# Regrouping the expert row gathers of a hybrid decoder step: U rows of the next slot ahead of the V rows of this one

## The chip, the cores and the metric

The kernel runs on one core of a Trainium2 chip. The metric is the device time in microseconds (us), the median of several runs. Engines are called as the profile calls them: PE (TensorE), DVE (VectorE), ACT (ScalarE), POOL (GpSimd), SP (SyncE).

## The reference

One decoder layer for 512 prompt tokens and 32 sample tokens (8 sequences of 4), model width 1024, everything in f32. Attention and retention are computed in parallel branches, the sample's attention over 4096 cached positions held in pages. What the change touches is the channel mixer behind them, in which each token picks 16 of 16384 experts for each of 8 heads and reads a row of 4 KB from each of two tables for every pick:

```python
def peer_block(h, w_q, sub_keys, u_tab, v_tab):
    ...
    s1, i1 = lax.top_k(s[:, :, 0], PEER_TOPK)
    s2, i2 = lax.top_k(s[:, :, 1], PEER_TOPK)
    ...
    top, flat = lax.top_k(cand, PEER_TOPK)
    e = ...
    g = jax.nn.softmax(top, axis=-1)
    u = u_tab[e]
    act = jax.nn.gelu(jnp.einsum('thkd,td->thk', u, h).astype(F32))
    return jnp.einsum('thk,thkd->td', (g * act).astype(h.dtype), v_tab[e])
```

At the end of the layer each token's x is gated: `x + sigmoid(rms_norm(x) @ w_ple_gate) * (p_emb @ w_ple)`.

## The kernel before

**Slots.** The expert work is cut into 34 slots (`SLOTS`): 8 for each of the four prompt tiles of 128 tokens (`BLOCKS`; one slot holds one head's or an equal share of picks), 2 for the 32 sample tokens. A slot is 16 gathers of U rows and 16 of V rows. Each gather (`gather`, L2127) is one indirect DMA of 128 rows of 4 KB, 512 KB, into one of 16 buffers (`ring`). The row numbers are columns of `IDX`.

**What a slot does.** DVE finds the top 16 (`dve_topk`). ACT makes the softmax's exponentials (`act_softmax`). PE turns the numbers and gates so that picks lie on partitions (`pe_turn_index`) and ACT copies them out of PSUM (`act_keep_index`). When a U row group has landed, DVE multiplies it with the hidden rows and sums (`dve_dots`, L2038, one call for each buffer). `dve_weights` makes gelu and gate into 32-column weight matrices `DG` (L2061), with one exponential from ACT in between (`act_gelu`, L2104; DVE waits for it at L2056). PE multiplies them with the V rows (`pe_weigh`, L2117), 16 matmuls for each of four groups `a` of four buffers, and adds into PSUM banks 6 and 7 over the eight slots of a tile; `dve_add` (L2073, L2075) adds these to x in `XB`.

**The ring.** In each buffer U(i), V(i), U(i+1), V(i+1) follow one another. V row group j of slot i is issued when dot j of slot i is done (`u_used`), the U rows of slot i+1 four at a time when weighing group a of slot i is done (`v_used`). All gathers stand in one queue, POOL's, in program order: 16 of V, then 16 of U. Among them at a block's end are the 16 small loads of h rows (`load_h_rows`, L2125), which wait for the store of h2 (L2173).

**The background.** Everything else, from the projections of later tiles to the sample's attention, is a generator on each engine (`pe_mixer`, `dve_mixer`, `act_mixer`), wrapped in `Background`. Each of its steps has a due position in slots (`STAGE_UNITS`, `PARTS_OF_TIME`, `when`): group 1 lies at -0.3 to 5.95, group 2 with the sample's retention at 6.02 to 14.2, the sample's attention over the cache (stage D, L794, L805, L865) at 14.25 to 26, the rest of the sample at 26.05 to 29.95. `mixer.until(s)` emits on this engine all steps due up to s, and then the slot's own work follows. So the positions set each engine's program order and nothing else: an engine does its instructions in that order and waits on semaphores where it has to.

PE before, for slot i: weighing group a at i + 0.1 + 0.1a, turning the index of slot i+2 at i + 0.5. DVE: weights at i, top-k of slot i+2 at i + 0.05, dot j of slot i+1 at i + 0.2 + 0.04j, the add of a finished tile at dot 10 (i + 0.6). ACT: exponential at i, softmax at i + 0.05, index copy at i + 0.5, store of a finished x at i + 0.65.

**The gating** of tile t (`pe_gating`, L1079 to L1108) has positions too (`GATE_SLOT`), 7 units for each tile: tile 0 at 30.1, tile 1 at 31.0, tile 2 at 32.0, tile 3 at 32.9 to 33.5, the sample (PT) at 33.7 to 33.9. Tile 3 and the sample need the sums of slots 31 and 33.

Of the kernel before, what the change touches and what calls it, by code (L numbers as in the profile page):

```python
# [209 lines left out]
GATE_SLOT = {0: (30.1, 31.0), 1: (31.0, 32.0), 2: (32.0, 32.9), 3: (32.9, 33.5), PT: (33.7, 33.9)}  # L210
# [40 lines left out]
def bass_decoder_step(nc, ins, outs, consts):  # L251
# [5 lines left out]
    with ctx:  # L257
# [48 lines left out]
        IDX = small(2, TOPK).bitcast(I32)  # L306
# [1671 lines left out]

        def first_of(i):
            return i == BLOCKS[BLOCK_OF[i]][1][0]  # L1980
# [50 lines left out]
        def dve_dots(dve, i, between):  # L2031
            p, blk = i % 2, BLOCK_OF[i]
            for j, (g, a) in enumerate(U_ORDER):
# [3 lines left out]
                dve.wait_ge(row_in[j], i * 32 + 16)  # L2037
# [50 lines left out]
        def act_keep_index(act, i):  # L2088
# [3 lines left out]
            act.activation(IDX[:, p, :].rearrange("p (g a) -> p g a", g=4), src[:, :, 0, :], ACT.Copy).then_inc(idx_put, 1)  # L2092
# [13 lines left out]
        def pe_weigh(pe, i, a):  # L2106
# [6 lines left out]
            for g in range(4):  # L2113
                pe.wait_ge(row_in[4 * a + g], i * 32 + 32)
# [12 lines left out]
        def gather(pool, table, i, j, g, a):  # L2127
            pool.indirect_dma_start(ring[j], None, table, bass.IndirectOffsetOnAxis(ap=IDX[:, i % 2, 4 * g + a:4 * g + a + 1], axis=0)  # L2128
                                    ).then_inc(row_in[j], 16)

        SMALL_LOADS = 10
        with nc.Block() as block:
# [207 lines left out]
            def _(pool):  # L2340
# [4 lines left out]
                for j, (g, a) in enumerate(U_ORDER):  # L2345
                    gather(pool, u_rows, 0, j, g, a)
                for i in range(SLOTS):
                    ends = last_of(i) and i + 1 < SLOTS
                    if ends:
                        t = BLOCKS[BLOCK_OF[i] + 1][0]  # L2350
                        pool.wait_ge(h2_stored, 16 * GROUPS[LATE_IN[t]].ln)
                    for j, (g, a) in enumerate(V_ORDER):
                        pool.wait_ge(u_used, i * 16 + j + 1)
# [3 lines left out]
                    if i + 1 < SLOTS:  # L2357
                        pool.wait_ge(idx_put, 2 * (i + 1) + 2)
                        for j, (g, a) in enumerate(U_ORDER):
                            if j % 4 == 0:  # L2360
                                pool.wait_ge(v_used, 4 * i + j // 4 + 1)
                            gather(pool, u_rows, i + 1, j, g, a)

            @block.tensor
            def _(pe):
# [5 lines left out]
                for i in range(SLOTS):  # L2371
                    for a in range(4):
                        mixer.until(i + 0.1 + 0.1 * a)
                        pe_weigh(pe, i, a)
                    if i + 2 < SLOTS:
                        mixer.until(i + 0.5)
                        pe_turn_index(pe, i + 2)
                mixer.until(SLOTS)

            @block.vector  # L2380
            def _(dve):
# [7 lines left out]
                for i in range(SLOTS):  # L2389
                    def between(j):  # L2390
                        mixer.until(i + 0.2 + 0.04 * j)
                        if j == 10 and last_of(i):
                            dve_add(dve, i)
# [7 lines left out]
                    else:  # L2401
                        dve_add(dve, i)
                mixer.until(SLOTS)

            @block.scalar
            def _(act):
# [14 lines left out]
                for i in range(SLOTS):  # L2421
# [3 lines left out]
                    if i + 2 < SLOTS:  # L2425
                        mixer.until(i + 0.05)
                        act_softmax(act, i + 2)
                        mixer.until(i + 0.5)
                        act_keep_index(act, i + 2)
# [42 lines left out]
```

## Time and profile before

| | |
|---|---|
| median of 3 runs | 2755.46 us (2750.58 to 2759.26) |
| profiled execution, own time | 2745.58 us |
| its span | 2743.5 us |
| PE, DVE, POOL busy | 1814.7, 1276.4, 1296.6 us |
| moved by DMA | 913.48 MB, mean 333 GB/s |
| gathers | 544 of U and 544 of V |

"Idle before, releaser" in a row of the trace is the time for which the engine stood still before the instruction and what ended it. Busy time of PE is what the profiler shows of pipelined matmuls. A wait is listed as the waiting engine and line, an arrow, and what released it.

### The profile page before, as it was taken

The numbers are of one execution on the slowest core, as the hardware profiler recorded it, in microseconds if no ns is written. First come the engines' busy times: TensorE is split into PE (matmuls) and PEld (weight loads), VectorE is DVE, ScalarE is ACT, GpSimd is POOL, SyncE is SP. The second block draws the span as 40 slices with busy tenths as digits, with TensorE's granted clock in tenths as the row PEclk, the third lists the DMA queues.
The fourth block names the chain that finished last, engine by engine and source line by source line (L and its number), as shares of the span: only waits on it lengthen the run. The fifth ranks groups of instructions, "written<-read, shape, count | busy, mean of one in ns | idle before, by whom it ended". The sixth has DMA issues, their size and how long they took to land.

```text
span 2743.5 us, 31504 instructions
## 1 busy us (share of the span) xinstructions
PE 1814.7 (66%) x10482; PEld 864.7 (32%) x10482; DVE 1276.4 (47%) x3210; ACT 497.6 (18%) x1061; POOL 1296.6 (47%) x1172
## 2 busy tenths in 40 slices
PE   6987687898965934787556666556665643364747
PEld 3443343343433412222233343333333310011212
DVE  1106664535354664644435354244342554664551
ACT  2112221101121100211122222222221200011121
POOL 0014634425545563645464542345235567876760
PEclk8998899999986965898878777767776766587878
DMA  6888958889968897999899999899899999999992
GB/s 210 279 263 308 388 182 337 312 302 368 396 241 293 314 359 270 367 355 398 340 347 380 383 342 343 322 397 355 316 350 356 361 402 386 384 405 405 346 375 79
DMA packets 338178, 913.48 MB, mean 333 GB/s; under 512 B 36865, under 2 KB 46242, under 8 KB 337378
## 3 DMA queue, kind: packets, MB, share of 16 engines
q0 software_dynamic: 160512, 580.99, 56.0%
q1 hardware_dynamic: 175250, 324.59, 33.2%
q10 hardware_dynamic: 2256, 5.90, 0.6%
q8 instruction: 85, 1.39, 0.2%
q14 instruction: 75, 0.61, 0.1%
HBM read 894.82 MB, written 16.52 MB: 332 GB/s over the span
## 4 chain that ended last, share of the span: by engine, by line
DMA 26%; PE 16%; POOL 8%; SPq 6%; issue 5%; DVE 4%; ACT 1%; DVEq 0%; ACTq 0%; POOLq 0%
DMA arena<-in_cache_v_dram 10%; POOL arena L2128 8%; DMA arena<-in_cache_k_dram 4%; SPq L2178 3%; PE ps L467 3%; SPq L2183 3%; PE ps L2117 3%; DMA arena<-in_peer_w_q_dram 3%; PE ps L794 2%; PE ps L1108 2%; DMA arena<-in_peer_u_dram,arena 2%; DMA arena<-in_peer_v_dram,arena 2%; PE ps L865 2%; DMA out_ret_sample_dram<-arena 2%; DMA arena<-in_w_in_dram 1%
## 5 line engine op out<-in xcount | busy, mean ns | idle before, releaser
L2128 POOL DMA_INDIRECT arena<-in_peer_u_dram,arena x544 | 615.3, 1131 | 994.2 <-PE ps L2117 804.8
L2038 DVE CUSTOM_DVE_ANT_0 arena<-arena 128x1024 f32<-128x1024 f32 x544 | 656.0, 1223 | 544.3 <-DMA arena<-in_peer_u_dram,arena 536.3
L467 PE MATMUL ps<-arena 128*128 128x512 f32 (+1 forms) x1472 | 686.9, 620 | 85.5 <-DMA arena<-in_peer_w_q_dram 30.9
L2128 POOL DMA_INDIRECT arena<-in_peer_v_dram,arena x544 | 640.6, 1178 | 202.9 <-issue 163.4
L467 PEld LDWEIGHTS ps<-arena 128*128 128x128 f32 (+1 forms) x1472 | 275.5, 193 | 471.0 <-issue 343.2
L2117 PE MATMUL ps<-arena 128*32 128x512 f32 x2176 | 322.3, 715 | 146.5 <-DMA arena<-in_peer_v_dram,arena 124.2
L794 PE MATMUL ps<-arena 128*128 128x128 f32 x1024 | 195.8, 353 | 209.5 <-DMA arena<-in_cache_k_dram 155.2
L794 PEld LDWEIGHTS ps<-arena 128*128 128x128 f32 x1024 | 154.8, 182 | 298.9 <-DMA arena<-in_cache_k_dram 158.5
L865 PE MATMUL ps<-arena 128*32 128x512 f32 x512 | 101.5, 876 | 152.6 <-DMA arena<-in_cache_v_dram 152.6
L1258 ACT ACTIVATE arena<-ps 128x512 f32<-128x512 f32 x256 | 143.4, 593 | 282.8 <-PE ps L794 282.5
L2117 PEld LDWEIGHTS ps<-arena 128*32 128x32 f32 x2176 | 71.5, 124 | 327.3 <-issue 300.9
L2125 POOL DMA_DIRECT2D arena<-h_for_experts x80 | 40.6, 523 | 188.4 <-DMA h_for_experts<-arena 188.4
L686 PE MATMUL ps<-arena 128*128 128x128 f32 (+1 forms) x360 | 57.6, 301 | 99.3 <-DVE arena L1920 34.5
L2056 DVE TENSOR_SCALAR arena<-arena 128x16 f32<-128x16 f32 x34 | 5.9, 175 | 219.1 <-ACT arena L2104 219.1
L805 PE MATMUL ps<-arena 128*32 128x128 f32 x2048 | 100.6, 360 | 1.3 <-ACT arena L1258 0.7
L686 PEld LDWEIGHTS ps<-arena 128*128 128x128 f32 (+1 forms) x360 | 46.1, 163 | 140.3 <-issue 66.9
L805 PEld LDWEIGHTS ps<-arena 128*32 128x32 f32 x2048 | 74.2, 145 | 20.8 <-issue 9.4
L1108 PE MATMUL ps<-arena 128*128 128x512 f32 (+1 forms) x160 | 72.1, 604 | 0.0
L865 PEld LDWEIGHTS ps<-arena 128*32 128x32 f32 x512 | 13.0, 129 | 173.8 <-DMA arena<-in_cache_v_dram 152.1
L2092 ACT ACTIVATE arena<-ps 128x16 int32<-128x16 f32 x34 | 6.3, 184 | 295.5 <-PE ps L2084 295.5
L477 PE MATMUL ps<-arena 128*32 128x512 f32 x288 | 50.6, 640 | 13.0 <-DMA arena<-in_w_a_up_dram 13.0
L1904 DVE TENSOR_TENSOR arena<-ps,arena 128x512 f32<-128x512 f32 (+1 forms) x20 | 13.7, 687 | 88.2 <-PE ps L467 88.2
(214 smaller groups left out, 1636.8 us busy)
## 6 DMA issues: line engine op xcount, KB each, us to landing
arena<-in_w_in_dram SPq DMA_DIRECT2D x156, 512.0 KB, 7.5
arena<-in_cache_k_dram SPq DMA_DIRECT2D x256, 256.0 KB
arena<-in_cache_v_dram SPq DMA_DIRECT2D x256, 256.0 KB
arena<-in_peer_w_q_dram SPq DMA_DIRECT2D x64, 512.0 KB, 12.6
arena<-in_w_out_dram SPq DMA_DIRECT2D x32, 512.0 KB, 10.1
arena<-in_w_b_up_dram SPq DMA_DIRECT2D x24, 512.0 KB, 6.6
arena<-h_for_experts POOLq DMA_DIRECT2D x80, 128.0 KB, 13.4
arena<-in_peer_u_dram,arena POOLq DMA_INDIRECT x544, 9.4
```

Source lines behind the costliest of these rows:

```text
L467: last = pe.matmul(bank[0:rows(t), :], x[:, c, cs], weight(pe, g.no, name, c), start=(c == 0), stop=(c == nd - 1))
L686: last = pe.transpose(bank[:, k * P:k * P + n], src[0:n, k * P:(k + 1) * P], ident[0:n, 0:n])
L794: last = pe.transpose(ps[:, hp % 2, k * P:(k + 1) * P], KP[i % 2][:, k, hp * P:(hp + 1) * P], ident)
L805: last = pe.matmul(ps[32 * k:32 * k + 32, 2, r * P:(r + 1) * P], Qb[:, p // 2 % 2, hp, :], KPT[:, r % 2, hp, k * P:(k + 1) * P], start=(hp ...
L865: last = pe.matmul(ps[32 * k:32 * k + 32, 3, :], AdT[:, r, 32 * k:32 * k + 32], VP[i % 2][:, k, :], start=(m == 0 and r == 0 and k > 0), s ...
L1108: last = pe.matmul(bank[0:n, :], XT[:, c, 0:n], WG[k][:, c, :], start=(c == 0), stop=(c == DC - 1))
L1258: act.activation(KPT[:, i % 2, hp, :], ps[:, hp % 2, :], ACT.Copy).then_inc(keys_kept, 1)
L2038: dve.tensor_tensor_reduce(ring[j], ring[j], HREP[:, g, :], 1.0, 0.0, ALU.mult, ALU.add, A16[:, p, 4 * g + a:4 * g + a + 1]).then_inc(u_us ...
L2117: last = pe.matmul(ps[32 * g:32 * g + 32, V_SUM + n, :], DG[:, p, 4 * g + a, :], ring[4 * a + g][:, n * 512:(n + 1) * 512], start=(first_o ...
L2128: pool.indirect_dma_start(ring[j], None, table, bass.IndirectOffsetOnAxis(ap=IDX[:, i % 2, 4 * g + a:4 * g + a + 1], axis=0)).then_inc(row ...
L2178: return sp.value_load(table[0:1, at:at + 1], min_val=0, max_val=ins["cache_k"].shape[1] - 1)
L2183: sp.dma_start(dst[:, k, :], pages[bass.ds(page(u // 4, u % 4, k), 1)].rearrange("a p d -> p (a d)")).then_inc(landed, 16)
```

## The change

The order in each buffer becomes U(0), U(1), V(0), U(2), V(1), U(3), and so on to V(32), V(33). V row group j of slot i is issued when dot j of slot i+1 is done; the U rows of slot i+2 when weighing group a of slot i is done. In the last slot, which has no dots beside it, V(33) is issued when the groups of slot 32 are weighed. `IDX` gets three buffers. On PE the weighing moves to i + 0.5 + 0.15a and the turning of the index ahead of it, to i + 0.45. On DVE the add of a finished tile moves from dot 10 of the tile's last slot to dot 1 of the next slot; the store of x on ACT follows it. The loads of h rows of the next tile come a slot earlier in POOL's queue. The gating of the sample moves to 33.97.

```diff
-GATE_SLOT = {0: (30.1, 31.0), 1: (31.0, 32.0), 2: (32.0, 32.9), 3: (32.9, 33.5), PT: (33.7, 33.9)}
+GATE_SLOT = {0: (30.1, 31.0), 1: (31.0, 32.0), 2: (32.0, 32.9), 3: (32.9, 33.5), PT: (33.97, 34.2)}
...
-        IDX = small(2, TOPK).bitcast(I32)
+        IDX = small(3, TOPK).bitcast(I32)
...
+        def u_landed(i):
+            return 16 * max(2 * i, 1)
+
+        def v_landed(i):
+            return 16 * min(2 * i + 3, 2 * SLOTS)
...
-                dve.wait_ge(row_in[j], i * 32 + 16)
+                dve.wait_ge(row_in[j], u_landed(i))
...
-                pe.wait_ge(row_in[4 * a + g], i * 32 + 32)
+                pe.wait_ge(row_in[4 * a + g], v_landed(i))
...
                 pool.wait_ge(idx_put, 2)
                 for j, (g, a) in enumerate(U_ORDER):
                     gather(pool, u_rows, 0, j, g, a)
+                pool.wait_ge(idx_put, 4)
+                for j, (g, a) in enumerate(U_ORDER):
+                    pool.wait_ge(u_used, j + 1)
+                    gather(pool, u_rows, 1, j, g, a)
                 for i in range(SLOTS):
-                    ends = last_of(i) and i + 1 < SLOTS
+                    ends = last_of(i + 1) if i + 2 < SLOTS else False
                     if ends:
-                        t = BLOCKS[BLOCK_OF[i] + 1][0]
+                        t = BLOCKS[BLOCK_OF[i + 1] + 1][0]
                         pool.wait_ge(h2_stored, 16 * GROUPS[LATE_IN[t]].ln)
                     for j, (g, a) in enumerate(V_ORDER):
-                        pool.wait_ge(u_used, i * 16 + j + 1)
+                        if i + 1 < SLOTS:
+                            pool.wait_ge(u_used, (i + 1) * 16 + j + 1)
+                        elif j % 4 == 0:
+                            pool.wait_ge(v_used, 4 * (i - 1) + j // 4 + 1)
                         gather(pool, v_rows, i, j, g, a)
                         if ends and j % 4 == 3:
                             load_h_rows(pool, t, j // 4)
-                    if i + 1 < SLOTS:
-                        pool.wait_ge(idx_put, 2 * (i + 1) + 2)
+                    if i + 2 < SLOTS:
+                        pool.wait_ge(idx_put, 2 * (i + 2) + 2)
                         for j, (g, a) in enumerate(U_ORDER):
                             if j % 4 == 0:
                                 pool.wait_ge(v_used, 4 * i + j // 4 + 1)
-                            gather(pool, u_rows, i + 1, j, g, a)
+                            gather(pool, u_rows, i + 2, j, g, a)
...
                 for i in range(SLOTS):
+                    if i + 2 < SLOTS:
+                        mixer.until(i + 0.45)
+                        pe_turn_index(pe, i + 2)
                     for a in range(4):
-                        mixer.until(i + 0.1 + 0.1 * a)
+                        mixer.until(i + 0.5 + 0.15 * a)
                         pe_weigh(pe, i, a)
-                    if i + 2 < SLOTS:
-                        mixer.until(i + 0.5)
-                        pe_turn_index(pe, i + 2)
-                mixer.until(SLOTS)
+                mixer.until(SLOTS + 1)
...
                     def between(j):
                         mixer.until(i + 0.2 + 0.04 * j)
-                        if j == 10 and last_of(i):
-                            dve_add(dve, i)
+                        if j == 1 and i and last_of(i - 1):
+                            dve_add(dve, i - 1)
...
-                    else:
-                        dve_add(dve, i)
-                mixer.until(SLOTS)
+                mixer.until(SLOTS - 0.05)
+                dve_add(dve, SLOTS - 1)
+                mixer.until(SLOTS + 1)
...
-                        mixer.until(i + 0.5)
+                        mixer.until(i + 0.45)
                         act_keep_index(act, i + 2)
-                    if last_of(i) and t < PT - 1:
-                        mixer.until(i + 0.65)
-                        act.wait_ge(x_added, 2 * BLOCK_OF[i] + 2)
-                        act.dma_start(xd[t * P:(t + 1) * P, :], XB).then_inc(xb_stored, 16)
+                    if i and last_of(i - 1) and BLOCK_OF[i - 1] < PT - 1:
+                        e = BLOCKS[BLOCK_OF[i - 1]][0]
+                        mixer.until(i + 0.5)
+                        act.wait_ge(x_added, 2 * BLOCK_OF[i - 1] + 2)
+                        act.dma_start(xd[e * P:(e + 1) * P, :], XB).then_inc(xb_stored, 16)
```

In `gather` and `act_keep_index` the row numbers' buffer `i % 2` becomes `i % 3`.

## Rows read from the trace of the kernel before

**Rows 1.** The page, span and transfer rate in 40 equal slices.

```profile
span 2743.5 us, 31504 instructions
...
GB/s 210 279 263 308 388 182 337 312 302 368 396 241 293 314 359 270 367 355 398 340 347 380 383 342 343 322 397 355 316 350 356 361 402 386 384 405 405 346 375 79
```

**Rows 2.** Windows of the three stages: length, busy us by engine, PE clock, DMA share, GB/s.

```profile
280.00:1349.00 1069.00, 799.56 (x3612) 360.50 (x3610) 549.13 (x1372) 175.88 (x363) 522.22 (x468) 0.86 0.87 327
1349.00:2129.00 780.00, 466.55 (x4363) 281.89 (x4361) 329.91 (x850) 189.29 (x399) 350.62 (x320) 0.73 0.96 351
2129.00:2672.00 543.00, 271.02 (x1665) 95.64 (x1665) 314.17 (x781) 65.67 (x159) 372.56 (x328) 0.72 1.01 384
```

**Rows 3.** Waits of the whole span: us in total, times, longest us.

```profile
POOL arena L2128 <- PE ps L2117: 804.8, 70, 41.0
DVE arena L2038 <- DMA arena<-in_peer_u_dram,arena: 536.3, 249, 27.4
...
DVE arena L2056 <- ACT arena L2104: 219.1, 34, 30.9
...
PE ps L2117 <- DMA arena<-in_peer_v_dram,arena: 124.2, 23, 22.7
```

**Rows 4.** Windows without and with gathers in turn, stage B.

```profile
1739.00:1780.00 41.00, 25.63 (x191) 14.48 (x190) 12.40 (x50) 10.29 (x21) 0.71 (x1) 0.64 0.84 297
1780.00:1834.00 54.00, 34.59 (x338) 20.69 (x337) 26.58 (x53) 13.67 (x29) 34.71 (x31) 0.74 0.98 376
1834.00:1863.00 29.00, 19.05 (x138) 11.58 (x139) 10.53 (x42) 5.65 (x13) 0.94 (x1) 0.59 0.88 322
1863.00:1917.00 54.00, 34.70 (x369) 20.46 (x367) 24.98 (x50) 13.28 (x28) 37.74 (x31) 0.78 1.01 383
```

**Rows 5.** Waits of PE and DVE at 230 to 900 and 900 to 1360.

```profile
PE ps L744 <- DVE arena L1642: 27.9, 2, 14.1
...
PE ps L686 <- DVE arena L1574: 19.4, 4, 8.9
...
PE ps L943 <- DVE arena L1808: 14.0, 1, 14.0
...
DVE arena L2038 <- DMA arena<-in_peer_u_dram,arena: 111.8, 55, 27.4
...
DVE arena L2038 <- DMA arena<-in_peer_u_dram,arena: 85.0, 37, 17.4
```

**Rows 6.** V gathers, median us to landing; then landing of all gathers (L2128).

```profile
arena<-in_peer_v_dram,arena POOLq DMA_INDIRECT x544, 12.0
...
DMA to landing us min/median/max: 4.3/10.7/22.0
```

**Rows 7.** Timeline of DVE and PE, in slots 4 and 20: start us, us.

```profile
634.23 1.22 DVE L2038 CUSTOM_DVE_ANT_0 arena<-arena 128x1024 f32<-128x1024 f32 x1
...
639.69 0.46 PE L2084 MATMUL ps<-arena 128*32 128x8 f32 x32
...
1875.57 1.23 DVE L2038 CUSTOM_DVE_ANT_0 arena<-arena 128x1024 f32<-128x1024 f32 x1 [0.72 <-DMA arena<-in_peer_u_dram,arena]
...
1890.11 0.44 PE L2084 MATMUL ps<-arena 128*32 128x8 f32 x32
```

**Rows 8.** Timeline of the tail, POOL and PE.

```profile
2660.65 0.93 POOL L2128 DMA_INDIRECT arena<-in_peer_u_dram,arena  x1 [0.30 <-issue]
...
2681.45 0.94 POOL L2128 DMA_INDIRECT arena<-in_peer_v_dram,arena  x1 [0.31 <-issue]
...
2652.66 1.93 PE L2117 MATMUL ps<-arena 128*32 128x512 f32 x16
...
2675.10 3.75 PE L1104 MATMUL ps<-arena 128*128 128x512 f32 x4 [11.74 <-ACT arena L1542]
...
2696.98 5.36 PE L2117 MATMUL ps<-arena 128*32 128x512 f32 x48
```

**Rows 9.** Timeline of SP's queue, the store of h2 of tiles 1 and 2.

```profile
675.34 1.72 SPq L2173 DMA_DIRECT2D h_for_experts<-arena  x2
```

More of the change, by code:

```diff
@@ L2091, in act_keep_index @@
             src = ps[:, 5, 0:32].rearrange("p (g c a) -> p g c a", g=4, c=2)
-            act.activation(IDX[:, p, :].rearrange("p (g a) -> p g a", g=4), src[:, :, 0, :], ACT.Copy).then_inc(idx_put, 1)
+            act.activation(IDX[:, i % 3, :].rearrange("p (g a) -> p g a", g=4), src[:, :, 0, :], ACT.Copy).then_inc(idx_put, 1)
             act.activation(GP[:, p, :].rearrange("p (g a) -> p g a", g=4), src[:, :, 1, :], ACT.Copy).then_inc(idx_put, 1)
@@ L2127, in gather @@
         def gather(pool, table, i, j, g, a):
-            pool.indirect_dma_start(ring[j], None, table, bass.IndirectOffsetOnAxis(ap=IDX[:, i % 2, 4 * g + a:4 * g + a + 1], axis=0)
+            pool.indirect_dma_start(ring[j], None, table, bass.IndirectOffsetOnAxis(ap=IDX[:, i % 3, 4 * g + a:4 * g + a + 1], axis=0)
                                     ).then_inc(row_in[j], 16)
@@ L2427, in _ @@
                         act_softmax(act, i + 2)
+                        mixer.until(i + 0.45)
+                        act_keep_index(act, i + 2)
+                    if i and last_of(i - 1) and BLOCK_OF[i - 1] < PT - 1:
+                        e = BLOCKS[BLOCK_OF[i - 1]][0]
                         mixer.until(i + 0.5)
-                        act_keep_index(act, i + 2)
-                    if last_of(i) and t < PT - 1:
-                        mixer.until(i + 0.65)
-                        act.wait_ge(x_added, 2 * BLOCK_OF[i] + 2)
-                        act.dma_start(xd[t * P:(t + 1) * P, :], XB).then_inc(xb_stored, 16)
+                        act.wait_ge(x_added, 2 * BLOCK_OF[i - 1] + 2)
+                        act.dma_start(xd[e * P:(e + 1) * P, :], XB).then_inc(xb_stored, 16)
                     if t and t != PT and i == BLOCKS[BLOCK_OF[i]][1][0] + 2:
@@ L2438, in _ @@
                         load_xb(t)
-                mixer.until(SLOTS)
+                mixer.until(SLOTS + 1)
 _INS = ["x_prompt", "x_sample", "cache_k", "cache_v", "state_ret", "page_table", "p_prompt", "p_sample",
```

## Prediction

> **What bounds the kernel now.** I read the stages in one table of windows first, then the waits of the whole span, then the waits of the first stage alone, then two slots in the timeline. The profiled execution spans 2743.5 us and took 2745.58 us, 0.36% under the median of 2755.46 us; the sum below is made against 2745.6 and the result is moved up by that 9.9 us. Anything within 0.3% (about 8 us) I call no change, since the three runs themselves spread over 8.7 us.
>
> [rows 2] cuts the slots into three stages. Stage A (280 to 1349 us, 14 slots) has PE busy 800 of 1069 us, DMA at 327 GB/s. Stage B (1349 to 2129, ten slots, the decode attention with its cache pages) has PE busy 467 of 780 us, DMA share 0.96, 351 GB/s. Stage C (2129 to 2672, nine slots) has PE at half its time and DMA share 1.01 at 384 GB/s. So A is set mostly by PE and by what PE waits for, B by transfers that come unevenly, C by transfers at their ceiling: the fastest slices of the page move 405 GB/s [rows 1].
>
> [rows 3] says how the ring of 16 buffers couples the engines. POOL sat idle 804.8 us until a weighing (L2117) freed ring buffers. DVE sat idle 536.3 us in the dots (L2038) until U rows landed: they are asked for only after the weighing of the slot and needed at once. DVE waited another 219.1 us for ACT's exponential at the start of the slots. PE waited only 124.2 us for V rows. Idle POOL is no loss in itself; it matters because transfers stop. [rows 4] shows it in stage B, slots 19 to 21: while gathers are issued the DMA moves 376 and 383 GB/s, mean 379.5, and in the stretches without gathers 297 and 322, weighted mean 307. The stretches without are 70 of 178 us, 39%.
>
> **The change, part by part.** No instruction of arithmetic and no gather is added: 544 + 544 gathers before and after, the same bytes. What changes is which row group sits in the ring beside which. Before: U(i), V(i), U(i+1). After: U(i+1), V(i), U(i+2), V(i+1). Each buffer still alternates, so no more rows are in flight; the slack is dealt out differently.
>
> *DVE and the U rows.* U(i+1) now has from the weighing of slot i-1 (positions 0.5 to 0.95 of that slot) until 0.2 of slot i, at least a quarter of a slot, some 19 us of a 76 us slot (1069/14); landing takes 10.7 us in the median [rows 6]. The 536 us leave L2038 nearly whole. Most of that isn't on the path, since DVE next waits for PE or for ACT. What is on it is PE waiting for DVE in stage A: [rows 5] has 27.9 + 19.4 + 14.0 = 61.3 us in the three largest such waits, where DVE itself had lost 111.8 + 85.0 us to U rows. I take half, **-30 us**; the bounds are 0 and the 269 us that PE idles in A, of which no more than about 100 are waits for DVE or ACT as short as these.
>
> *PE and the V rows.* V(i) now follow the dots of slot i+1 (0.2 to 0.8) and are weighed at 0.5, 0.65, 0.8, 0.95. For the first group that is 0.5 - 0.32 = 0.18 slot: 14 us of a 76 us slot, 14 us of a 78 us slot in B, 11 us of a 60 us slot in C. V rows take 12.0 us where their landing was waited for [rows 6]. That is tight. [rows 7] measures it: in slot 4 the dot that would release the fourth V row ends at 634.23 + 1.22 = 635.5 and PE reaches position 0.5 (L2084) at 639.7, a slack of 4.2 us; in slot 20 it is 1876.8 against 1890.1, 13.3 us. Both were measured with DVE held up by U rows, which now goes away, and what the first group waits the later ones need not wait again. Bounds: nothing (slot 20's slack widened by the U waits gone) and 12.0 - 4.2 = 7.8 us a slot. I take the value nearer to slot 20, since eased DVE moves that way: 1.5 us a slot in A, 14 x 1.5 = **+21 us**, nothing in B, where DVE waits for ACT and is ahead. In C PE is half idle and a late V row costs only if the ring stops.
>
> *The transfers in B.* A gather stretch without stops: V issued at the pace of the dots, U at the pace of four weighings spread over 0.45 slot. What is left without gathers is from about 1.0 to 1.2, some 16 us in 78. By the two rates of [rows 4] the mean becomes (16 x 307 + 62 x 379.5)/78 = 365 GB/s, and 780 x 351/365 = 750: **-30 us**. Bounds: none, and everything at 379.5, -59 us. PE's own cache waits shrink with it and are in this term, not beside it; stage A's weight and state loads may gain alike, for which I take **-10 us** (0 to -30).
>
> *A ceiling stated elsewhere.* The trace's slices reach 405 GB/s and stage C holds 384 for 543 us [rows 1, 2]. The Trainium skill, "DMA: Bandwidth & Descriptors", section "Where 436 GB/s comes from", says that for transfers between HBM and SBUF the HBM side binds at about 358 GB/s for each core. By that rule B at 351 would be full and its term -15 us at most, C's nothing. The trace disagrees as to this core running alone.
>
> *C.* 543 us at 384; at 404 it would be 516, the bound of -27. The issue order is as dense as before, and the dots now wait behind the top-k instead of behind U rows. I take **-5 us**.
>
> *The tail.* Before, V(32) is the last batch of gathers but two, now the last but one: weighing slot 32 moves behind dots(33). Before, it ended at 2652.66 + 1.93 and the gating of tile 3 ran to 2697 on PE while V(33) landed; their last issue is at 2681.45, the last weighing at 2696.98, and after its 5.36 us 2743.5 - 2702.3 = 41 us of the sample's gating follow [rows 8]. After, V(32) can't be issued before the place of U(33), last at 2660.65; plus 12 us landing and 2 us the weighing of slot 32 ends near 2675, 20 us later. Gating 3, whose body starts at position 32.9 behind the third group, shifts by about 15 of these, and the weighing of slot 33 (1.93 + 5.36 = 7.3 us) now stands whole behind it, where its first group was interleaved. **+14 us**, bounds 0 (gather stream earlier by as much) and +25.
>
> *Edits at nothing.* The third row-number buffer: 16 words, no instruction. Index turning 0.05 earlier and ahead of the weighing: the top-k it needs lies at 0.05. The 16 loads of h rows at a block's end move one slot up on POOL, and behind them the V gathers; the h2 of tiles 1 and 2 was on its way to memory by 677 us [rows 9], while slot 6 lies near 280 + 6 x 76 = 736; for the sample the position (before 29.95) is ahead of slot 30. If that cover went, POOL's whole queue would stand, and with it every engine within a slot. The adds to XB move to 0.24 of the next slot, ahead of PE's 0.5 which waits for them; the ACT queue's store follows at 0.5, its reload at 2.7. First U(1) ahead of V(0): V(0) has until 0.5.
>
> Sum: -30 + 21 - 30 - 10 - 5 + 14 = -40 us on 2745.6, that is 2705.6; on the median of the runs **2715 us**, 1.5% faster.
>
> **The rivals.**
> *Slower: V rows late in PE's ordered queue.* Place: each first group in stage A. All work of PE, projections too, stands behind the wait. For it: slot 4's 4.2 us; the engines of A are the ones with nothing to spare. Against: DVE is relieved at the same time. Price at 7.8 us a slot: 14 x 7.8 = 109 us instead of 21, so the sum is +48: 2803 us. It decides from (21 + 40)/14 = 4.4 us of wait a slot on. Chance 0.27.
> *No change: the transfers are the bound and no deeper.* The ring holds what it held, so the U rows' slack is paid by V's, and B's gaps only move. For it: DMA share 0.96 and 1.01 in B and C. Against: 307 against 379.5 GB/s. B, C and the loads then give nothing, and of the sum stands -30 + 21 + 14 = +5: 2755.5 + 5 = 2760 us. Chance 0.15. (By the Trainium skill's 358 GB/s, above, this would be the likeliest case: -15 for B added, 2745 us.)
> *Faster by more: A's stalls go and B runs level.* -60 for A, V waits nothing, B -59, loads -20, C -10, tail +5: -144, 2611 us. For it: POOL's 804.8 us. Against: the chain needs all at once. Chance 0.18.
> That the change doesn't do what it says I hold unlikely: the positions are in the program text and DVE's waits follow from the order.
>
> **How the numbers follow.** Forecast 0.40, more 0.18: faster 0.58. No change 0.15. Slower 0.27. The forecast's own range, with V's waits from 0 to 4 us a slot and B from 0 to -59, is 2665 to 2745. For 8 in 10 I reach halfway into the faster case and to the price of the slower one: 2635 to 2805.
>
> **What would show it.** DVE's wait at L2038 for U rows below 100 us of 536. POOL's wait for L2117 no longer in pieces of 28 us but of under 12. B's windows level, near 365 GB/s, its ten slots in 750 us. PE's wait at L2117 for V rows between 60 and 200 us, mostly in C. The last weighing later than 2696.98 less what was gained before it, and 41 us after it. Wrong if the V waits stand in A with over 4 us a slot, if B's rate stays at 351, or if gains in B are less than the tail loses.

## The result and the profile after

The changed kernel takes 2733.4 us in the median (2727.9 to 2742.7), the kernel before 2751.9 beside it, ratio 0.9936 (95% interval 0.9912 to 0.9961); each side has six runs. In a second set (below) the ratio was 0.9969 (0.9951 to 0.9987). So it is faster by 0.3 to 0.6%, where 1.5% was forecast. The profiled execution was the slowest of its six, 2742.72 us with a span of 2740.7.

The page of the changed kernel, span and rate in 40 slices, beside [rows 1]:

```profile
span 2740.7 us, 31504 instructions
...
GB/s 211 280 260 310 292 269 322 349 313 333 331 297 264 334 361 331 271 356 390 321 277 382 377 390 369 355 373 352 399 359 326 376 406 389 407 394 405 290 363 147
```

Its waits over the whole span, beside [rows 3] (L2136 is the gather, L2046 the dots, L2125 the weighing, L2064 DVE's wait for ACT):

```profile
POOL arena L2136 <- DVE arena L2046: 674.3, 103, 31.6
...
DVE arena L2064 <- ACT arena L2112: 334.1, 33, 54.9
PE ps L2125 <- DMA arena<-in_peer_v_dram,arena: 314.3, 54, 22.9
...
POOL arena L2136 <- PE ps L2125: 184.6, 30, 24.6
...
DVE arena L2046 <- DMA arena<-in_peer_u_dram,arena: 53.1, 27, 13.7
```

Each coupling moved as the change is written. DVE waits 53 us for U rows instead of 536. POOL waits for dots and weighing in 133 pieces, 859 us together; before, it waited 850 us in 79 pieces, nearly all for the weighing. DVE's waits did not all go away: those for ACT's exponential grew from 219 to 334 us. The price stands in the third row: PE waits 314 us for V rows, 190 more than before.

The windows from slot 0 to 14, 14 to 23 and 23 to 33, cut at the same calls of `dve_weights` as [rows 2] (columns as there):

```profile
281.00:1363.00 1082.00, 810.67 (x3606) 363.36 (x3605) 540.94 (x1371) 175.97 (x363) 532.64 (x465) 0.86 0.87 321
1363.00:2110.00 747.00, 449.14 (x4364) 263.59 (x4366) 324.13 (x850) 188.71 (x400) 346.23 (x311) 0.74 0.98 359
2110.00:2679.00 569.00, 281.62 (x1665) 98.18 (x1657) 310.14 (x782) 66.58 (x160) 379.88 (x339) 0.70 1.00 379
```

The middle stretch went from 780 to 747 us, 351 to 359 GB/s. (It is nine slots and the last stretch ten; the prediction had it the other way round, which moves none of its terms by more than 2 us.) The first grew by 13 us, the last by 26. But cuts by slots flatter a kernel that lets the slots of stage B run ahead of the background beside them. Fixed points of the background are fairer, and they stand in SP's queue: the load of the page table (stage B can begin), the last load of cache values (its end), the load of tile 0's gate weights (every earlier stage drained), the end of the span. Windows of before between these points:

```profile
280.00:1355.00 1075.00, 803.54 (x3646) 361.42 (x3644) 554.71 (x1401) 176.85 (x367) 524.79 (x471) 0.86 0.87 325
1355.00:2233.00 878.00, 523.37 (x4880) 307.34 (x4880) 381.68 (x966) 206.94 (x435) 403.13 (x365) 0.73 0.97 357
2233.00:2488.00 255.00, 113.58 (x696) 32.23 (x696) 151.82 (x393) 15.73 (x52) 191.74 (x159) 0.70 1.02 394
2488.00:2743.00 255.00, 148.56 (x574) 53.43 (x574) 113.25 (x259) 43.65 (x95) 133.68 (x132) 0.77 0.80 294
```

And of after:

```profile
280.00:1369.00 1089.00, 812.51 (x3615) 364.44 (x3613) 547.48 (x1402) 177.22 (x367) 536.11 (x468) 0.86 0.87 320
1369.00:2235.00 866.00, 511.85 (x4888) 291.24 (x4888) 384.65 (x987) 206.00 (x437) 419.00 (x373) 0.73 0.98 363
2235.00:2496.00 261.00, 117.33 (x704) 32.78 (x704) 162.30 (x436) 16.73 (x55) 191.19 (x163) 0.69 1.03 399
2496.00:2741.00 245.00, 150.31 (x590) 53.78 (x590) 90.14 (x194) 43.32 (x92) 122.52 (x122) 0.78 0.78 288
```

Start to page table +14, cache pages -12, from there to the gate weights +6, from those to the end -10. What follows tells which of these four are of the kernel, since one execution may differ from the next of the same kernel by as much.

### The profile page after: what moved, and what is told of

Same layout as the page of the kernel before. It is cut to its first block, busy times and chain, and to the rows that moved or that the text cites. A ratio compares the mean times of both kernels' runs of the same rounds, so it can differ in the third digit from the quotient of the medians.

```text
span 2740.7 us, 31504 instructions
## 1 busy us (share of the span) xinstructions
PE 1817.4 (66%) x10482; PEld 851.2 (31%) x10482; DVE 1259.0 (46%) x3210; ACT 497.5 (18%) x1061; POOL 1312.1 (48%) x1172
## 4 chain that ended last, share of the span: by engine, by line
DMA 25%; PE 19%; POOL 8%; issue 6%; SPq 6%; DVE 4%; ACT 2%; DVEq 0%; ACTq 0%; POOLq 0%
POOL arena L2136 8%; DMA arena<-in_cache_v_dram 6%; DMA arena<-in_peer_v_dram,arena 6%; DMA arena<-in_cache_k_dram 5%; PE ps L467 4%; PE ps L2125 4%; SPq L2186 3%; PE ps L1108 3%; SPq L2191 3%; PE ps L794 2%; DMA arena<-in_w_ple_gate_dram 2%; DMA arena<-in_w_in_dram 1%; PE ps L865 1%; DMA out_ret_sample_dram<-arena 1%; DMA arena<-in_peer_w_q_dram 1%
## 5 line engine op out<-in xcount | busy, mean ns | idle before, releaser
L2136 POOL DMA_INDIRECT arena<-in_peer_v_dram,arena x544 | 728.8, 1340 | 816.0 <-DVE arena L2046 674.3
L2136 POOL DMA_INDIRECT arena<-in_peer_u_dram,arena x544 | 542.6, 997 | 373.4 <-PE ps L2125 177.1
L2046 DVE CUSTOM_DVE_ANT_0 arena<-arena 128x1024 f32<-128x1024 f32 x544 | 638.1, 1221 | 63.2 <-DMA arena<-in_peer_u_dram,arena 53.1
L2125 PE MATMUL ps<-arena 128*32 128x512 f32 x2176 | 350.5, 769 | 314.3 <-DMA arena<-in_peer_v_dram,arena 314.3
L794 PE MATMUL ps<-arena 128*128 128x128 f32 x1024 | 183.1, 337 | 175.5 <-DMA arena<-in_cache_k_dram 156.5
L2125 PEld LDWEIGHTS ps<-arena 128*32 128x32 f32 x2176 | 75.4, 129 | 508.0 <-issue 507.0
L794 PEld LDWEIGHTS ps<-arena 128*128 128x128 f32 x1024 | 145.4, 173 | 267.6 <-DMA arena<-in_cache_k_dram 157.9
L865 PE MATMUL ps<-arena 128*32 128x512 f32 x512 | 98.6, 852 | 134.8 <-DMA arena<-in_cache_v_dram 134.8
L2064 DVE TENSOR_SCALAR arena<-arena 128x16 f32<-128x16 f32 x34 | 6.7, 197 | 345.1 <-ACT arena L2112 334.1
L805 PE MATMUL ps<-arena 128*32 128x128 f32 x2048 | 92.0, 336 | 0.7 <-ACT arena L1258 0.7
```

The source lines that it names most:

```text
L794: last = pe.transpose(ps[:, hp % 2, k * P:(k + 1) * P], KP[i % 2][:, k, hp * P:(hp + 1) * P], ident)
L805: last = pe.matmul(ps[32 * k:32 * k + 32, 2, r * P:(r + 1) * P], Qb[:, p // 2 % 2, hp, :], KPT[:, r % 2, hp, k * P:(k + 1) * P], start=(hp ...
L865: last = pe.matmul(ps[32 * k:32 * k + 32, 3, :], AdT[:, r, 32 * k:32 * k + 32], VP[i % 2][:, k, :], start=(m == 0 and r == 0 and k > 0), s ...
L2046: dve.tensor_tensor_reduce(ring[j], ring[j], HREP[:, g, :], 1.0, 0.0, ALU.mult, ALU.add, A16[:, p, 4 * g + a:4 * g + a + 1]).then_inc(u_us ...
L2125: last = pe.matmul(ps[32 * g:32 * g + 32, V_SUM + n, :], DG[:, p, 4 * g + a, :], ring[4 * a + g][:, n * 512:(n + 1) * 512], start=(first_o ...
```

## The experiments

Thirteen more runs were made, in four sets, each set with the kernel before beside it. Two of them repeat a kernel: "again" is the changed kernel, and "new_order_best" is "later_and_earlier" once more. In the table, "P." (load of the page table), "C." (last load of cache values), "G." (load of tile 0's gate weights) and "end" are the profiled execution's times of the four points in us, "G. to end" the last stretch.

| kernel | ratio (95% interval) | P. | C. | G. | end | G. to end |
|---|---|---|---|---|---|---|
| before | | 1355 | 2233 | 2488 | 2743.5 | 255 |
| after | 0.9936 (0.9912 to 0.9961) | 1369 | 2235 | 2496 | 2740.7 | 244 |
| again | 0.9969 (0.9951 to 0.9987) | 1362 | 2225 | 2485 | 2731.8 | 247 |
| gate0_later | 0.9999 (0.998 to 1.0019) | 1359 | 2227 | 2489 | 2743.0 | 254 |
| weigh_later | 0.9783 (0.9754 to 0.9812) | 1320 | 2185 | 2452 | 2689.6 | 238 |
| dots_later | 0.9904 (0.9877 to 0.9931) | 1333 | 2215 | 2466 | 2720.2 | 254 |
| later_in_a | 0.9814 (0.9786 to 0.9843) | 1317 | 2184 | 2446 | 2693.7 | 248 |
| later_from_b | 0.9933 (0.9907 to 0.9959) | 1358 | 2223 | 2490 | 2724.9 | 235 |
| weigh_later_still | 0.9772 (0.9748 to 0.9797) | 1321 | 2183 | 2443 | 2678.0 | 235 |
| dots_earlier | 0.9864 (0.9837 to 0.9892) | 1351 | 2208 | 2470 | 2704.2 | 234 |
| tail_alone | 0.9968 (0.9952 to 0.9985) | 1367 | 2255 | 2512 | 2752.5 | 241 |
| later_and_earlier | 0.9759 (0.9733 to 0.9785) | 1328 | 2186 | 2444 | 2683.0 | 239 |
| dots_half_slot | 0.9808 (0.9782 to 0.9833) | 1312 | 2175 | 2425 | 2683.2 | 258 |
| old_order_best | 0.979 (0.9751 to 0.9829) | 1321 | 2191 | 2445 | 2693.9 | 249 |
| new_order_best | 0.9753 (0.9719 to 0.9787) | 1321 | 2184 | 2444 | 2678.4 | 234 |

**First set.** The changed kernel again:

> The changed kernel once more, beside the others of this set. Theory 1 (late V rows on PE and a stop before slot 30 give back what stage B gains) and its rivals all expect the same here: a ratio near 0.994. It is the yardstick for the three others, and its profile is a second reading of the stages: slots 0 to 14 longer than before by 10 us or more, slots 14 to 24 shorter by about 30 us, and the gap before slot 30 again over 60 us from index to index, if these are of the kernel and not of one execution.

The order of the stages recurred only in part. Slots 0 to 14 were 5.8 us longer, not 10; slots 14 to 23 shorter by 36; from slot 30's weights to slot 31's 82 us, as in the first profile (83), where before had 54.

For that gap the profile had a suspect. PE's timeline of the changed kernel shows tile 0's first gate matmul and the weighing of slot 30 behind it:

```profile
2539.26 3.78 PE L1104 MATMUL ps<-arena 128*128 128x512 f32 x4 [34.72 <-DMA arena<-in_w_ple_gate_dram]
...
2559.00 3.64 PE L2125 MATMUL ps<-arena 128*32 128x512 f32 x32
```

```diff
-GATE_SLOT = {0: (30.1, 31.0), 1: (31.0, 32.0), ...}
+GATE_SLOT = {0: (30.8, 31.3), 1: (31.3, 32.0), ...}
```

> The changed kernel with the gating of tile 0 at positions 30.8 to 31.3 and of tile 1 at 31.3 to 32.0 in place of 30.1 to 31.0 and 31.0 to 32.0, so that the weighing of slot 30 stands ahead of the wait for the gate weights on PE. Theory 1: PE's 34.7 us wait at L1104 held the V rows of slot 30 in the ring and stopped the gathers; with it gone the run is 20 to 30 us faster than the changed kernel (ratio to before near 0.985), and POOL has no stop over 10 us at slot 30. Rival: the gather stream loses nothing there that it doesn't catch up, or the gating chain of five tiles sets the end; then the time is within 5 us of the changed kernel, or slower because gating starts later.

The theory fell. The run is slower than the changed kernel by 0.3%, with intervals that overlap at their ends. The wait only changed its name, as the same stretch of this run shows: PE now waits 39 us for V rows, and tile 0's gate matmuls start 20 us later.

```profile
2533.93 3.64 PE L2125 MATMUL ps<-arena 128*32 128x512 f32 x16 [39.34 <-DMA arena<-in_peer_v_dram,arena]
...
2559.25 1.96 PE L1104 MATMUL ps<-arena 128*128 128x512 f32 x4 [2.03 <-ACT arena L1542]
```

PE stood from 2494.6 us on. The first V gather of slot 30 was issued only at 2501.06, since in the new order 16 U gathers of slot 31 stand ahead of it in POOL's queue, and SP's loads of the gate weights, 4 MB, were on their way. The gathers issued between 2495 and 2536 us whose landing the trace has took 23.8 to 29.4 us, and from 2490 to 2534 us the DMA share was 1.04 at 381 GB/s. So the stop is one of transfers; whether the order in POOL's queue or the 4 MB has the greater part in it was not tried. The gating behind it is a chain in which a late start is not made up in full: gate 0 to end took 201 us in the changed kernel, 184 here with gate 0 starting 70 instead of 43 us after its weights were asked for.

The weighing 0.1 slot later:

```diff
-                        mixer.until(i + 0.5 + 0.15 * a)
+                        mixer.until(i + (0.6 if i + 1 < SLOTS else 0.5) + 0.15 * a)
                         pe_weigh(pe, i, a)
```

> The changed kernel with the weighing at i + 0.6 + 0.15a in place of i + 0.5 + 0.15a (slot 33 as it was). Theory 1: late V rows stand in PE's ordered queue; 0.1 slot more is 7 us more slack, PE's waits for V rows in stage A (115 us in the changed kernel) fall under 50 us and the run is 20 to 50 us faster than the changed kernel. Rival: PE would have stood idle there anyway, for DVE, ACT or weights; the V waits fall but others grow by as much, and the time stays within 8 us. It could also be slower, if U rows asked for later make DVE wait again (L2046 for U rows over 150 us).

This gives 2.2% against before, 48 us under "again", at the good end of what was expected. The page table is asked for at 1320 us instead of 1362. The V waits of PE in A fell less than expected, from 118 to 82 us.

And the order of before with later dots:

```diff
-                        mixer.until(i + 0.2 + 0.04 * j)
-                        if j == 10 and last_of(i):
+                        mixer.until(i + 0.35 + 0.04 * j)
+                        if j == 6 and last_of(i):
                             dve_add(dve, i)
```

> The kernel before, its order of gathers kept, with dot j at i + 0.35 + 0.04j in place of i + 0.2 + 0.04j and the add of a finished tile at dot 6 in place of dot 10 (the same position within 0.01). It gives the U rows 0.15 slot more without touching the V rows' slack. Theory 1: what the change gives is DVE freed from U rows and a more even stream, and both are to be had without the reordering and without late V rows: DVE's wait for U rows falls from 536 us to under 200, PE's for V rows stays near 124, and the run is at least as fast as the changed kernel, 20 to 50 us under before. Rival: only the reordering gives the gain, since here the weights still come after the last dot: the later dots delay weights and weighing and the run is slower than before by up to 30 us.

The old order with later dots was faster than the change, 0.9904 against 0.9969 in the same set. DVE's wait for U rows fell to 307 us (under 200 had been expected). PE's for V rows moved little, from 124 to 147:

```profile
DVE arena L2038 <- DMA arena<-in_peer_u_dram,arena: 306.7, 145, 18.4
...
PE ps L2117 <- DMA arena<-in_peer_v_dram,arena: 146.5, 25, 22.9
```

So freeing DVE from a good part of its waits for U rows needs no reordering.

**Second set.** Where does the later weighing pay? The condition on `i` is all that differs (`i < 14`, then `14 <= i < SLOTS - 1`), then 0.7 for 0.6.

> The changed kernel with the weighing 0.1 slot later in slots 0 to 13 alone (0.6 + 0.15a there, 0.5 + 0.15a from slot 14 on). The later weighing everywhere took 42 us out of stage A's end (slot 14 at 1313.7 us against 1355.6) and another 9 us later. Theory 1 (late V rows in PE's queue cost where PE is the engine with nothing to spare): stage A gives its 35 to 42 us here too, B and C stay as in the changed kernel, ratio to before 0.981 to 0.985. Rival: what a stage gains is given back in B and C, because the gather stream there is bound by transfers and only starts earlier; then the whole is 20 us or less faster than the changed kernel (ratio above 0.989).

> The complement: the weighing 0.1 slot later in slots 14 to 32 alone. Theory 1: PE waits only 20 to 35 us for V rows in stage B and is half idle in C, so the gain is small, 5 to 15 us over the changed kernel, and slot 14 is reached at 1355 to 1363 us as in the changed kernel; the gains of this run and of its complement add up to the 48 us of both together. Rival (a stage's gain is given back): this one alone gives 30 us or more, since the end is set by the late stages.

Stage A alone gives 0.9814, nearly all; from B on 0.9933, which is not told apart from the changed kernel. Against "again" the two take 1.55 and 0.36 points, together 1.9, and both at once (weigh_later) took 1.9. So they add as far as the intervals tell, and the rival, by which later stages give a gain of A back, fell: it wanted a ratio above 0.989 for A alone.

> The weighing at i + 0.7 + 0.15a (slot 33 as it was), another 0.1 slot. Theory 1: the slack of a first group was 18 us in the median and 1.5 at the least in stage A with 0.6; most of it is covered, so another step gives little: within 12 us of the run with 0.6, PE's waits for V rows in A under 60 us, DVE's waits for U rows over 120 us. Rival (PE does better for other reasons than late V rows, as its background work standing earlier): the gain goes on, 20 us or more below the run with 0.6.

0.9772 against 0.9783, which is within 12 us, as theory 1 had it. DVE's waits for U rows came back to 131 us over the whole span. PE's waits in stage A (230 to 1310 us) show the row still falling:

```profile
PE ps L2125 <- DMA arena<-in_peer_v_dram,arena: 47.7, 9, 10.0
```

The cross-check leaves PE alone and asks for the rows earlier: `mixer.until(i + 0.1 + 0.04 * j)`.

> The changed kernel, weighing where it was (0.5 + 0.15a), with dot j at i + 0.1 + 0.04j in place of i + 0.2 + 0.04j: the V rows are asked for 0.1 slot earlier without anything moved on PE. Theory 1: it is the V rows' slack that counts, so this gives much the same as the later weighing: 25 to 50 us faster than the changed kernel, PE's waits for V rows in A under 90 us instead of 116. Rival (it is PE's order that counts): within 10 us of the changed kernel. It could be slower, because dots stand ahead of DVE's background work that PE waits for.

0.9864, 28 us under the changed kernel, with the V waits in A at 69 us. Slack made on DVE works too, so it is the slack and not only PE's order; but it gives 28 us where the later weighing gave 48. In this profile A gained 11 us, cache pages another 6, the stretch from the gate weights to the end 13; the first two are no more than one profile can say (third set). The waits of PE in A show what is lacking: the V rows take 49 us less than in "again", while waits for DVE are 95 us instead of 75 and those for other transfers 80 instead of 59. DVE's background, which the earlier dots now precede, fits the first of these; no run separates it.

**Third set.** The tail's part of the change on the kernel before:

```diff
-GATE_SLOT = {..., PT: (33.7, 33.9)}
+GATE_SLOT = {..., PT: (33.97, 34.2)}
...
-                    else:
-                        dve_add(dve, i)
-                mixer.until(SLOTS)
+                mixer.until(SLOTS - 0.05)
+                dve_add(dve, SLOTS - 1)
+                mixer.until(SLOTS + 1)
```

> The kernel before with nothing of the change but its end: the last add moves on DVE from the start of slot 33 to position 33.95, behind tile 3's gating, and the sample's gating to 33.97. Theory: the tail, forecast 14 us longer, was 9 to 10 us shorter from the last index on, because DVE no longer stands in that add (30.8 us before) while tile 3's gating waits behind it; then this run is 5 to 10 us faster than before, all of it after 2671 us, and tile 3's last DVE step (L1957) ends about 5 us earlier. Rival: the tail was shorter only because gathers and weighings came otherwise; then there is no difference from before (within 3 us).

0.9968 (0.9952 to 0.9985), about 9 us: as much as the whole change gave in the set of "again". DVE and PE at the end of this run, the last step of tile 3's gating, the add, and the sample's first matmul:

```profile
2717.36 0.69 DVE L1957 TENSOR_TENSOR arena<-arena 128x512 f32<-128x512 f32 x1
2721.04 1.29 DVE L2073 COPY arena<-ps 128x512 f32<-128x512 f32 x2 [2.99 <-PE ps L2117]
...
2720.90 0.30 PE L1079 MATMUL ps<-arena 32*128 32x32 f32 x2
```

Tile 3's y (L1957) is done before the last weighing ends, so its store and SP's load of the sample's p behind it were through when PE came to L1079, and that row has no wait. From the end of the last weighing to the end of the span this kernel takes 31.6 us. That stretch divides all the profiles of this study: the three kernels without this part take 40.7 to 41.2 us there, the kernels with it 31.6 to 33.3. Up to slot 33 this kernel is the one before, and still its profiled execution asked for the page table at 1367 us and not 1355, and for the last cache values 22 us later. (Its profiled execution, 2754.5 us, was the slowest of its twelve. Of the 12 us up to the page table, 9 are PE's own busy time, 812.6 us from 280 us on where before had 803.5.) That is how little one profile says of a stage: differences under some 12 us in A or B are not read from one execution here.

> The weighing at i + 0.7 + 0.15a, and from slot 14 on also the dots 0.1 slot earlier (i + 0.1 + 0.04j). Each step alone: 0.7 gave 66 us under before, 42 of them before stage B; earlier dots took 6 us more out of stage B. Theory 1 (slack of V rows only pays where PE waits for them): in B PE waits 1 us for V rows with 0.7, so the two don't add, and this run is within 6 us of the run with 0.7. Rival (earlier dots level the transfers of B further): 6 to 15 us faster than it, stage B (from the page table's load to the last cache load) at 855 us or less instead of 862.

0.9759 against 0.9772: the two steps don't add by more than the intervals. Stage B took 858 us, between the two expectations.

> The kernel before, its order of gathers kept, with dot j at i + 0.5 + 0.03j and the add of a finished tile at dot 3. U rows have 0.3 slot more than before. If the order of before can give what the changed order gives once its positions suit it, this is 40 us or more under before and stage B near 862 us. If the reordering has a gain of its own (weights stand ready long before their V rows, gathers go on over the slot's boundary), this stays at 15 to 30 us under before, as with 0.35 + 0.04j, and B stays near 880 us. It could be slower than that run, for the last dots now press on the weights: then POOL's waits for the weighing grow again over 620 us.

```diff
-                        mixer.until(i + 0.2 + 0.04 * j)
-                        if j == 10 and last_of(i):
+                        mixer.until(i + 0.5 + 0.03 * j)
+                        if j == 3 and last_of(i):
```

The old order reaches 0.9808, 53 us under before, with 862 us in stage B: both as expected if the old order can give what the new one gives. Its waits over the whole span, beside [rows 3]:

```profile
POOL arena L2128 <- PE ps L2117: 566.2, 71, 38.3
...
DVE arena L2038 <- DMA arena<-in_peer_u_dram,arena: 197.6, 103, 16.6
...
PE ps L2117 <- DMA arena<-in_peer_v_dram,arena: 148.5, 23, 22.9
```

**Fourth set.** Both orders at their best, on one chip:

> The kernel before, its order of gathers kept, with the two parts that paid by themselves there: dots at i + 0.5 + 0.03j (0.9808) and the end of the changed kernel (0.9968). If the two add, this is at 0.978 of before, about 60 us, with the page table's load near 1312 us, the last cache load near 2175 and about 241 us from the gate weights' load to the end. Theory: the reordering itself is worth little or nothing; what pays is slack for U rows and the tail, so this lies within 0.3% of the best reordered kernel. Rival: the reordering is worth 10 us or more once its V rows have slack; then the reordered kernel beside it is faster by that.

> The fastest reordered kernel so far (weighing at i + 0.7 + 0.15a, dots 0.1 slot earlier from slot 14 on, 0.9759) once more, on the same chip as the best kernel with the old order. Expected at 0.974 to 0.978 again. Theory: within 0.3% of the old order's best. Rival: 10 us or more below it.

The old order's best takes 2696.0 us (2675.5 to 2699.5, six runs), the new order's 2680.5 us (2677.4 to 2685.0, five runs), ratios 0.979 (0.9751 to 0.9829) and 0.9753 (0.9719 to 0.9787) with overlapping intervals. That leans to a gain of the reordering of its own of some 10 to 15 us, and does not settle it. Up to the gate weights both take the same 2444 to 2445 us; where they differ in the profile is behind them, 249 against 234 us, and from the last weighing to the end both take 32 to 33. Whether the tail's part adds to the later dots is not told either (0.979 against 0.9808 for the dots alone, in another set). The new order's best is 68 us under the kernel before of its set, 2.5%.

## Why the prediction was wrong in size

The sum was -30 + 21 - 30 - 10 - 5 + 14 = -40 us. Measured were -18 and -10. By SP's fixed points, in the profiles of "after" and "again", the forecast's -19 us for stage A (-30, +21 and -10) came out as +14 and +7, B's -30 as -12 and -15, C's -5 as +6 and +5, the tail's +14 as -11 and -8. The couplings between the engines moved as forecast; the sizes in A and B did not, and of the tail the mechanism was missed too. That the sign came out right is in part luck: tail_alone took 9 us off without any reordering, in a stretch where I had expected a loss, and "again" as a whole took 10. The reordering without its tail part was not run; what is left for it is some 9 us by the first set and nothing by the second.

**The V rows in PE's queue, forecast +21 us.** This is the step that failed. PE's waits in the changed kernel, from 230 to 1310 us, the largest and two others:

```profile
PE ps L2125 <- DMA arena<-in_peer_v_dram,arena: 115.2, 17, 21.5
...
PE ps L966 <- DMA arena<-in_state_ret_dram: 22.7, 4, 8.3
PE ps L686 <- DVE arena L1574: 18.1, 4, 9.5
```

Before, V rows had 34.6 us of that:

```profile
PE ps L2117 <- DMA arena<-in_peer_v_dram,arena: 34.6, 5, 10.9
```

The growth is 81 us, 5.8 us a slot against the 1.5 I took, above the 4.4 from which the slower rival was to decide. It has two parts.

First groups: they waited 62.5 of the 115 us. From the end of dot 3 to PE's arrival (the start of the weighing less its idle time) the first groups of slots 0 to 13 had 13.3 us in the median, near the 14 us of the positions, but four of the fourteen had 3.0 us or less, and in one of them PE came 3.6 us before the dot was done. I read the slack from two slots and took the value near the better one, on the ground that eased DVE would widen it. In slot 20 it did, from 13.3 to 22.6 us; in slot 4 it fell from 4.2 to 1.2. A queue waits for each late case and gets nothing for the early ones, so it is the spread that counts and not the middle.

Later groups: the prediction put them at nothing ("what the first group waits the later ones need not wait again"). They waited the other 52.7 us, all in slots 6 to 12. The positions would have warned: by them the four groups have 0.18, 0.17, 0.16 and 0.15 slot, so the last has the least.

**DVE's relief, forecast -30 us.** Undersized too, which is why the change didn't become slower. All waits of PE listed for 230 to 1310 us, summed by what ended them (up to 7 us in "all" are waits without a releaser):

| us | V rows | DVE | ACT | other transfers | all |
|---|---|---|---|---|---|
| before | 35 | 123 | 29 | 86 | 273 |
| after | 115 | 78 | 20 | 63 | 281 |
| again | 118 | 75 | 22 | 59 | 279 |
| weigh_later | 82 | 70 | 17 | 77 | 250 |
| weigh_later_still | 48 | 78 | 21 | 93 | 244 |
| dots_earlier | 69 | 95 | 19 | 80 | 269 |
| dots_half_slot | 50 | 72 | 36 | 84 | 242 |

The change takes 45 us of waits for DVE (forecast: half of 61), 9 for ACT and 23 for transfers (forecast 10), and puts 81 in their place. The sum stays, and so does the stage: 14 and 7 us longer in two profiles is about what tail_alone's unchanged part shows. Counted from 280 us to each kernel's own load of the page table, PE is idle for 272 us before, 277 and 276 in the changed kernel's two profiles, 240 in weigh_later, 231 in weigh_later_still and 229 in dots_half_slot. Give the V rows slack and the waits for DVE and ACT stay low while the 81 us shrink: that is weigh_later. Some of the transfer waits come back then; that PE is at its weights earlier would explain it, and was not followed up.

**The transfers in B, forecast -30 us.** By slots -33 and -36, which looks exact. By SP's fixed points it was 878 us before, 866 and 863 after, so 12 to 15 us: half the term. The rate after is what the working gave (363 GB/s, forecast 365), but the whole stage had 357 before and not the 351 of the prediction's window, so less was to be had. Twelve us alone would be within what one profile can say, but the table bears them out: all ten profiles of the new order take 856 to 868 us from page table to cache values, the three of the old order with the dots at 0.2 or 0.35 take 877 to 888. With the dots at 0.5 the old order takes 862 and 870, so this gain needs no reordering either. That the stream is more even shows in slot 21 of the changed kernel, before its V rows are issued, while they are, and while U rows follow:

```profile
1932.00:1945.00 13.00, 5.17 (x49) 3.25 (x49) 11.56 (x42) 1.55 (x5) 5.37 (x7) 0.63 1.03 402
1945.00:2001.00 56.00, 36.43 (x380) 22.53 (x376) 23.34 (x47) 16.48 (x33) 18.94 (x15) 0.80 0.98 363
2001.00:2021.00 20.00, 13.20 (x92) 5.20 (x92) 2.58 (x10) 2.76 (x6) 12.18 (x13) 0.68 1.03 401
```

In this slot no stretch is left like the pauses of [rows 4], 29 to 41 us at 297 to 322 GB/s. Over all of stage B (page table to cache values) POOL still stands nearly as long as before for dots and weighing, 358 us against 382, but in 42 pieces of at most 25.5 us and not in 27 of up to 41.0.

**C, forecast -5 us.** 5 to 6 us longer from the last cache values to the gate weights, with DMA at 399 GB/s against 394. The rate was already near the fastest seen here, 403 to 405, and the 5 us were not to be had.

**The tail, forecast +14 us.** Wrong in sign: 8 to 11 us shorter. The weighing of slot 33 did end later (2709.0 against 2702.3), but the sample's gating behind it took 32 instead of 41 us, which I had carried over as a constant. Before, DVE and PE:

```profile
2702.40 1.29 DVE L2073 COPY arena<-ps 128x512 f32<-128x512 f32 x2 [30.76 <-PE ps L2117]
...
2706.79 0.69 DVE L1957 TENSOR_TENSOR arena<-arena 128x512 f32<-128x512 f32 x1
...
2709.93 0.42 PE L1079 MATMUL ps<-arena 32*128 32x32 f32 x2 [7.59 <-DMA arena<-in_p_sample_dram]
```

After:

```profile
2703.64 0.69 DVE L1957 TENSOR_TENSOR arena<-arena 128x512 f32<-128x512 f32 x1
2709.03 1.29 DVE L2081 COPY arena<-ps 128x512 f32<-128x512 f32 x2 [4.71 <-PE ps L2125]
...
2708.90 0.30 PE L1079 MATMUL ps<-arena 32*128 32x32 f32 x2
```

Before, DVE stood 30.76 us in the add of slot 33 with tile 3's gating behind it in the queue; the y of tile 3, its store and the load of the sample's p came late, and PE waited 7.59 us for it. The change moves that add behind the gating. The prediction looked at PE and POOL there and not at what DVE's queue held. tail_alone shows the mechanism by itself.

**The range.** The forecast's own range of 2665 to 2745 us does not follow from its bounds: with 4 us a slot (+35) and B at nothing (+30) its upper end is 2780.

**The rivals.** "Slower" had its mechanism right, and its size of 4.4 us a slot was passed; what it lacked was DVE's relief of 54 us (45 for DVE, 9 for ACT) in place of 30, and the tail. "No change" was near in size, for the wrong reason: in A and B it is not a ceiling of transfers. Between the last cache values and the gate weights the changed kernel held 399 GB/s for 261 us, and weigh_later_still 403 for 260, the third of its windows:

```profile
280.00:1321.00 1041.00, 809.68 (x3615) 367.17 (x3613) 548.47 (x1402) 176.89 (x367) 536.54 (x466) 0.87 0.89 333
1321.00:2183.00 862.00, 519.57 (x4848) 303.56 (x4848) 384.27 (x988) 207.31 (x436) 408.75 (x366) 0.72 0.98 364
2183.00:2443.00 260.00, 115.57 (x716) 33.41 (x720) 162.94 (x434) 16.86 (x55) 194.53 (x164) 0.70 1.03 403
2443.00:2678.00 235.00, 156.20 (x622) 55.91 (x614) 91.52 (x196) 43.36 (x92) 135.95 (x131) 0.81 0.84 314
```

The Trainium skill, "DMA: Bandwidth & Descriptors", section "Where 436 GB/s comes from", lets the HBM side bind at about 358 GB/s. The measurement decides against that here, with the one core running.

**The checks named ahead.** DVE's wait for U rows under 100 us: right (53). POOL's pieces for the weighing under 12 us: wrong for the longest (24.6); the average is 6 us, but it was 11.5 before and decides little. B's windows near 365 GB/s: 363. PE's V waits between 60 and 200 us, mostly in C: wrong in size, 314 us; 166 of them stand in C (2110 to 2679 us), but 115 in A. The sign of being wrong, over 4 us a slot in A, came: 115 us are 8.2 a slot. B's ten slots in 750 us: 747, for nine. The tail 41 us: wrong, 32.

## What to carry to other kernels

When slack is moved from one engine's operand to another's, look at which queue the new wait stands in and at the whole spread of the slack over the slots, not at its nominal value or one good slot: here the same reordering was worth 0.3 to 0.6% with 0.18 slot of slack on PE and 2.3% with 0.38 (the tail's 0.3% is in both). Look at every group and not only the first. Before reordering a ring, move the consumer in the old order: 0.15 slot more for the U rows gave 1.0%, and 0.15 to 0.3 slot gave 1.9%, by two lines. And take a bundle apart: an add that moved behind a gating by the way gave 0.3%, as much as the rest of the change together in one of its two measurements.

## What the runs showed that I had not expected

A gather of 512 KB issued behind 16 others and beside 4 MB of weights took 23.8 to 29.4 us to land (slot 30 of gate0_later), where the median landing before was 10.7 us [rows 6], and PE waited 39.34 us in one piece for such rows. And two executions of the same program part differ by 12 to 24 us at fixed points over 2500 us, though all 23 times of before in the first set lie within 0.8%.
